# A two-block transformer on one core: where the second half of an expert's rows is scattered and added

## What is computed

```python
def moe_swiglu(h, router_w, w1, w3, w2):
    ...
    top_vals, top_idx = lax.top_k(logits, TOP_K)
    top_w = jax.nn.softmax(top_vals, axis=-1)
    gates = jnp.sum(jax.nn.one_hot(top_idx, N_EXPERTS, dtype=jnp.float32) * top_w[..., None], axis=1)
    ...
    for e in range(N_EXPERTS):
        a = t @ w1[e]
        b = t @ w3[e]
        out = out + gates[:, e:e + 1] * ((jax.nn.silu(a) * b) @ w2[e])
```

## Time and profile before

| | us |
|---|---|
| Median of 3 runs | 3105.84 |
| Lowest, highest | 3100.02, 3113.47 |
| The profiled execution | 3106.7 |
| Its span | 3104.9 |

### The profile page before, as it was taken

The page is one execution under the profiler, slowest core; times in us unless marked ns, Lnnn a source line. Parts: engine busy times, 40 slices in busy tenths (PEclk is TensorE's granted clock), DMA queues, the critical chain, the costliest instruction groups (busy, mean ns, idle before and its releaser), DMA issues.

```text
span 3104.9 us, 34324 instructions
## 1 busy us (share of the span) xinstructions
PE 2898.1 (93%) x13334; PEld 2376.6 (77%) x13334; DVE 2062.2 (66%) x2910; ACT 1696.0 (55%) x2271; POOL 32.9 (1%) x55
## 2 busy tenths in 40 slices
PE   8998899999887999999999989989899999898998
PEld 6887688788765878777877768877778788776786
DVE  5566655656664898889888955468655455587553
ACT  5645354555523777677767754455454444555543
POOL 0000000000001000000000000000000000000000
PEclk9998899999987999999999989999999999999999
DMA  6443455454333999999989965544455555444453
GB/s 220 149 135 114 132 178 188 155 166 140 122 128 112 350 349 333 323 333 345 330 318 344 343 234 183 187 143 153 146 170 185 170 189 187 144 162 149 157 186 112
DMA packets 173658, 633.63 MB, mean 204 GB/s; under 512 B 19521, under 2 KB 19521, under 8 KB 173489
## 3 DMA queue, kind: packets, MB, share of 16 engines
q1 hardware_dynamic: 170752, 621.88, 59.0%
q0 software_dynamic: 2736, 9.49, 0.9%
HBM read 629.20 MB, written 2.10 MB: 203 GB/s over the span
## 4 chain that ended last, share of the span: by engine, by line
PE 78%; DVE 12%; DMA 4%; ACT 4%; issue 1%; SPq 0%; DVEq 0%; ACTq 0%; POOLq 0%
PE ps L1306 24%; PE ps L1308 23%; PE ps L1307 23%; DVE wlo L737 4%; DMA raw<-in_W 4%; PE ps L1418 2%; DVE CA L1182 2%; ACT whi L301 1%; PE ps L1495 1%; PE ps L1542 1%; PE ps L1338 1%; PE ps L1405 0%; PE ps L1404 0%; DVE XN L905 0%; DVE Z L1269 0%
## 5 line engine op out<-in xcount | busy, mean ns | idle before, releaser
L737 DVE TENSOR_TENSOR wlo<-raw,whi 128x1024 fp32r<-128x1024 f32 x1182 | 1394.0, 1221 | 560.4 <-ACT whi L301 550.8
L301 ACT ACTIVATE whi<-raw 128x1024 fp32r<-128x1024 f32 x1182 | 1197.8, 1057 | 600.8 <-PE ps L1308 547.7
L1306 PE MATMUL ps<-whi,XH 128*128 128x512 f32 (+1 forms) x2192 | 873.4, 398 | 41.2 <-DVE XL L755 17.3
L1307 PE MATMUL ps<-wlo,XH 128*128 128x512 f32 (+1 forms) x2192 | 859.0, 392 | 0.0
L1308 PE MATMUL ps<-whi,XL 128*128 128x512 f32 (+1 forms) x2192 | 859.0, 392 | 0.0
L1306 PEld LDWEIGHTS ps<-whi,XH 128*128 128x128 f32 x2192 | 418.8, 191 | 134.9 <-DVE XL L755 21.8
L1308 PEld LDWEIGHTS ps<-whi,XL 128*128 128x128 f32 x2192 | 417.6, 191 | 87.5
L1307 PEld LDWEIGHTS ps<-wlo,XH 128*128 128x128 f32 x2192 | 418.9, 191 | 82.8 <-issue 0.5
L1306 PE MATMUL ps<-whi,XEH 128*128 128x512 f32 x704 | 284.2, 404 | 1.4 <-DVE XEL L986 1.4
L1308 PE MATMUL ps<-whi,XEL 128*128 128x512 f32 x704 | 278.4, 395 | 0.0
L1307 PE MATMUL ps<-wlo,XEH 128*128 128x512 f32 x704 | 278.0, 395 | 0.0
(11 more groups left out here) (358 smaller groups left out, 2467.9 us busy)
## 6 DMA issues: line engine op xcount, KB each, us to landing
raw<-in_W SPq DMA_DIRECT2D x1182, 512.0 KB, 5.2
GP<-in_ffn_post_g POOLq DMA_DIRECT2D x4, 512.0 KB, 4.0
X<-in_x SPq DMA_DIRECT2D x1, 1024.0 KB, 5.0
skew<-RB POOLq DMA_DIRECT2D x4, 256.0 KB, 2.8
RB<-skew POOLq DMA_DIRECT2D x8, 128.0 KB, 2.5
GP<-in_mix_post_g POOLq DMA_DIRECT2D x2, 512.0 KB, 3.8
out<-X SPq DMA_DIRECT2D x1, 1024.0 KB, 4.0
mload<-in_cum_sums POOLq DMA_DIRECT2D x1, 768.0 KB, 8.5
```

What stands on the lines that cost most here:

```text
L301: act.activation(k.whi[:, slot, part], k.raw[:, slot, part], ACT.Copy).then_inc(*k.up("act_hi"))
L737: dve.tensor_tensor(k.wlo[:, slot, part], k.raw[:, slot, part], k.whi[:, slot, part], ALU.subtract).then_inc(*k.up("dve_lo"))
L1306: pe.matmul(ps, xh, k.whi[:, slot, cols], start=first, stop=False)
L1307: pe.matmul(ps, xh, k.wlo[:, slot, cols], start=False, stop=False)
```

## The change

The callback that `up` is given is called behind the first two groups and not only the first, and is told which; it scatters tile 0 behind group 0, as before, and tile 1 behind group 1. The call that scattered tile 1 behind the whole of `up` is gone, on TensorE and on VectorE. The waits for the two adds stay where they were, ahead of `down`. ScalarE's program is the same.

```diff
--- before.py
+++ after.py
@@ -949,8 +949,8 @@
             if g:
                 self.turn(T, g - 1, tiles)
             self.gate(T, g, tiles, norm)
-            if g == 0 and after_first:
-                after_first()
+            if g < NT and after_first:
+                after_first(g)
 
     def down(self, T, tiles, between=None):
 
@@ -1009,9 +1009,7 @@
             self.gathered(T, 0, c)
         for e in range(NE):
             U = f"{T}.e{e}"
-            self.up(U, 1, None, (lambda: self.scatter(T, e - 1, 0)) if e else None)
-            if e:
-                self.scatter(T, e - 1, 1)
+            self.up(U, 1, None, (lambda t: self.scatter(T, e - 1, t)) if e else None)
             self.down(U, 1, lambda j: self.place(T, e, j, POS))
             dve.wait_ge(*k.at(f"{U}.yh"))
             dve.scalar_tensor_tensor(out=k.YL[:], in0=flat(k.ps[:, 4:6, :]), scalar=k.gslot, in1=k.YH[:], op0=ALU.mult, op1=ALU.subtract).then_inc(*k.up("dve_split", f"{U}.yl"))
@@ -1508,8 +1506,8 @@
                 self.slab(self.columns(half, tiles * (g % 3), XH, XL, tiles), f"{T}.mm{g}" if half else None)
             if g:
                 self.turn(T, g - 1, tiles)
-            elif after_first:
-                after_first()
+            if g < NT and after_first:
+                after_first(g)
 
     def down(self, T, tiles, between=None):
 
```

## The result

The changed kernel takes 3085.49 us, the median of 5 runs (3082.72 to 3086.36), beside 3111.87 us for 5 runs of the kernel before (3100.02 to 3113.47). The ratio is 0.9918, with a 95% interval of 0.9904 to 0.9931: 0.8% faster. The profiled execution took 3082.7 us, with a span of 3080.9 where the one of before had 3104.9: 24.0 us less.

What follows compares the result with a forecast made beforehand. The prediction saw TensorE at 93% of the span, pausing in experts 1 to 7 only for the add. 18.2 (waits) + 4.7 (clock) - 1.4 (late next) = 21.5 us off 3106.7 gave 3085, range 3078 to 3098.

Steps and rivals of the forecast that it cites:

- the waits: End of up, experts 1 to 7: TensorE's waits for the add before down go, 18.2 us gained with matmul start spacing.
- the clock: Expert stage: the three falls to 1.2 GHz go with the pauses and vanish, 3 x 1.55 = 4.7 us gained.
- what is late next: Turn behind the first down slab: TensorE waits for the last group's GN, 0.2 us in each of seven experts, 1.4 lost.
- The 101.5 and 101.6 us: Experts 1 to 7: the time each would take with the pause gone, about 101.5 us, or 101.6 as a sign.
- the rival with a chance of 0.16: Expert stage: the falls of the clock stay, at even distances of 208 us; gain only 16.8 us, 3090; chance 0.16.
- The second group: Behind up's second group: the add delays the `wlo` run 0.9 us, TensorE comes 1.0 later, margin 1.6; cost 0.
- The transfers: Experts 1 to 7: transfers keep up without the pause, the down projection refilling the lead; nothing charged.
- The scatter: Tile 1's four scatter matmuls cost TensorE the same behind the second group as at the end of up, 4 x 0.23 + 0.08.
- the lateness of VectorE: Turn and second down slab: late VectorE and transfers show up there, up to 13 us of the 21; 3098; chance 0.11.
- the pauses only move: Expert stage: no change, the seven pauses only move since transfers set the pace; 3106; chance 0.06.
- the ring of three slots: Up projection: slower, TensorE waits on ring laps if landings average over 6.3 us; 3122; chance 0.05.

Runs made afterwards that it cites:

- the kernel with two operations more: The changed kernel with two more VectorE operations of the add's size, results unused, before the add of tile 1 behind the second group: 3089.68 us, ratio 0.9934.
- The first experiment: The kernel before with only tile 1's four scatter matmuls moved behind the second group, VectorE's add left at the end of up: 3117.21 us, ratio 1.0033.
- add doubled: The kernel before with one more VectorE operation of the add's size, result unused, just before the add of tile 1: 3121.19 us, ratio 1.0040.
- the short pause: The changed kernel with one VectorE operation of the add's size behind group 5 of up, TensorE waiting for it before group 6: 3113.45 us, ratio 1.0021.

## Why the prediction was right

The measured time is 3085.5, the forecast 3085, from 3078 to 3098. The mechanism was right, and so were the terms for the waits and the clock; one term, what is late next, was mis-sized. That the number fits to half a microsecond is luck: the profiled execution gained 24.0 us where 21.5 were forecast, and its time, 3082.7, lies 2.8 us below the median of the changed kernel. Of the 24.0 us between the two spans, 23.0 lie between the first and the last slab's start of the stage (821.4 and 798.4 us), and 1.0 outside, which no step explains.

*The waits, 18.2 us.* The up projections of experts 1 to 7 take 476.3 us before and 458.3 after (7 x 65.47): 18.0. That the cost of a wait is to be read from the starts and not from the idle time was needed for this: the idle times give 16.5. The 101.5 and 101.6 us that the prediction gives for an expert do not follow from its own sum, which takes some 3.1 us from a mean of 103.8 (experts 1 to 6) and leaves 100.7; measured is 100.78. Neither number enters the sum.

*The clock, 4.7 us.* The down projections of experts 3 and 5 went from 36.88 and 36.87 to 35.31, that of expert 7, up to its last slab, from 30.50 to 28.94: 4.7. The row of before for expert 7:

```profile
1785.33:1815.83 30.50, 30.50 (x128) 24.55 (x129) 23.14 (x21) 19.03 (x21) 0.00 (x0) 0.94 0.88 302
```

The experiments settle what the trace of before had left open, the rival with a chance of 0.16: pauses put in the middle of up bring falls there, and without pauses there are none. The clock of the changed kernel is 1.00 up to the last scatter of the stage; the fall there, at 1799.9, goes with the wait behind expert 7 and is not among the terms. By the rule of the Trainium skill that the prediction weighed (TensorE: Matmul & The Clock Gate, part HAM oscillation) a long enough idle gap brings the half level, and the runs agree in that: the fifteen longest of 38 pauses all went with a fall. That the longest gap is hit first, which I had drawn from it, the trace of before contradicts (2.0 us with a fall, 3.2 without), and two other kernels do too (2.5 with a fall in both, 3.0 and 2.7 without).

*What is late next, 1.4 us back.* This is the term that failed: nothing was lost there. In the profile after, GN of the last group ends 0.7 to 1.4 us before the turn asks for it in experts 1 to 7. I had taken 0.2 us for each, between 0 and expert 0's 0.40, and expert 0 does not stand for the others. Read expert by expert, the trace of before already gives less: GN ends 1.3, -0.1, 1.1, -0.1, 0.6, 1.3 and 0.1 us before the turn would ask for it, 0.3 us of waits in all. Other kernels show that the term can be real: with both adds behind group 0, three experts paid 1.7 us (2.2 by the starts). With the wait alone moved GN was 1.2 to 2.4 us early, of which 1.0 is the scatter that still stands ahead of the turn there. I put the differences down to single landings; that is argued from one profiled execution of each kernel and not tested. Expert 0 lost 0.26 us less than before as well, for no reason in the change.

*The second group, 0.* As worked out, to a tenth: the `wlo` run later by 0.9, TensorE later by 1.0, 1.6 us of margin left; and the kernel with two operations more gives the same margin (2.3 added, 0.65 come through).

*The transfers, 0.* The stretch in up moves 361 GB/s at a share of 1.00, that of before 359 at 0.99, and the down projection takes the slack. An expert's share is 0.96 to 0.97, as forecast. The landings came out at a median of 6.0 us, under the 6.3 from which the prediction has TensorE wait, though single ones, up to 7.6, are over it. In the kernel with two operations more the median is 6.6, and there the waits for `wlo` stand.

*The scatter, "the same in its new place".* In TensorE's own time, yes. The first experiment adds what that sentence left out: in its old place it was mostly hidden behind VectorE's lateness, so moving it without the add costs.

The rivals: the falls stay, no; the lateness of VectorE shows up behind in some kernels (up to 1.1 us at one turn), but not in this one; the pauses only move, no; the ring of three slots, no, though 2.3 us more of delay at the new place bring out waits of up to 1.7 us. That it is the ring that hands them on is argued from the landings, and no kernel with another ring was run.

The ratio, 0.8%, is a little more than the forecast 0.7%, most of it because the three runs of before shown first had a lower median (3105.84) than all five (3111.87) or the 23 of the first series of experiments (3107.79).

## What to carry to other kernels

Where an engine waits for another's late step, ask first what the waiting instruction needs of it. Here moving one `wait_ge` to the first instruction that overwrites the banks gave as much as the whole change (ratio 0.9926 and 0.9918, with overlapping intervals), without moving a single operation. And move both halves of a step or neither: here the producer's half alone took work out of a mostly hidden place and made the kernel 0.3% slower. Price a pause of TensorE by the distance of its starts, and add what the clock takes behind it, here a quarter as much again.

## What the runs showed of the hardware

Of the 38 pauses in the table, the 5 shortest (1.3 to 1.9 us) went without a fall to 1.2 GHz, 14 of the 18 next (2.0 to 3.3 us) went with one, and so did the 15 longest (up to 5.9 us). Within the middle group the length alone does not decide (2.04 us with a fall, 3.25 us without, both in one execution); what does is open. The fall begins between 3.1 us before the end of the pause and 1.5 us behind it. It takes 3.4 or 6.8 us. One of 3.4 costs 1.55 us in the down projection; one of 6.8 there costs 2.8 (matmuls alone and add doubled).

The times of kernels with pauses spread more: 3100 to 3120 in the 23 runs of before in the first series, 3109 to 3119 in 8 with the short pause, against 3082.7 to 3086.4 in 5 runs of the changed kernel and 3081 to 3087 in the six of each of the kernels with the add at other places. That the varying pauses and falls are the cause fits this, but it was not tested by itself.
